# A two-layer decoder trunk on one core: v held in TensorE and the turned probabilities moved, so that y and its gates come out turned

## The chip, the cores and the metric

The kernel runs on one core of one Trainium2 chip. Its time is device microseconds of that core: 276.67 us, the median of three runs (276.58 to 276.71). Times below are read from one profiled execution of it.

## What is computed

One sequence of 256 positions with 1024 channels passes through two layers, with an RMS norm before each and after the last. All numbers are float32.

```python
def even_layer(hn, w_in, w_out, ln_g, ln_b, w_s, b_s):
    z = hn @ w_in
    u, v, g_a, q, k, vv, g_b = jnp.split(z, cuts, axis=-1)
    y_a = chunked_gmlp(u, v, ln_g, ln_b, w_s, b_s) * jax.nn.silu(g_a)
    y_b = moba_attention(q.reshape(hs), k.reshape(hs), vv.reshape(hs)).reshape(Bn, S, B_WIDTH)
    return jnp.concatenate([y_a, y_b * jax.nn.silu(g_b)], axis=-1) @ w_out

def odd_layer(hn, w_in, w_out):
    q, k, v, g = jnp.split(hn @ w_in, [C_WIDTH, 2 * C_WIDTH, 3 * C_WIDTH], axis=-1)
    y = dilated_mixture(q.reshape(hs), k.reshape(hs), v.reshape(hs)).reshape(Bn, S, C_WIDTH)
    return (y * jax.nn.silu(g)) @ w_out
```

With 256 positions the attention of the even layer (8 heads of 64 channels) is plain causal attention, and that of the odd layer (16 heads) is causal attention with a weight of 1, 2, 3 or 0 for each distance, which is a mask added to the scores.

## The kernel before

**Products.** Each of the four weight matrices is loaded in halves (512 rows by 512 columns, 1 MB) into three slots of `w_raw`. A quarter (two chunks of 128 rows) is split in two parts: ScalarE (ACT) copies it to `w_hi` in a rounded type (step `round`, L602) and VectorE (DVE) subtracts to get `w_lo` (step `rest`, L740). Nine quarters fit. TensorE (PE) makes each product of three: high by high, low by high, high by low. An item is one quarter for one group of two PSUM banks, and it is issued in two steps ("product n.0" and "n.1"), one for each chunk. Groups of kind value, gate, gelu and residual hold weights still and positions on partitions come out: hnT is stationary and 512 weight columns move (L1000 to L1002, six matmuls a chunk). Queries and keys come out turned, channels on partitions: the weights are stationary and the 256 positions move (L959 to L963, twelve matmuls a chunk).

**Attention of a head n** passes through these steps, each of which stands in the list of every engine that has a part in it: `scores` (four matmuls into a bank; then DVE adds the mask, scales and takes the least, L873; then ACT takes the exponential and the sum `den`, L652), `transpose` (PE turns three 128x128 blocks of `probs`, L911; ACT copies them to `probsT`, L660), and for every two heads `values` (PE, L1042 to L1044: turned probabilities stationary, 64 columns of v moving, six matmuls; DVE takes the reciprocal of the sums, L880, and multiplies by it into y, L882). Two `probs` buffers and two `probsT` buffers are used in turn. After four pairs `gating` multiplies y by the gate, and `y_pair` turns y for the output product: four transposes by PE, then ACT makes `yT_hi` (L664) and DVE `yT_lo` (L890).

**Order.** Nothing is scheduled at run time. `steps()` writes one list; each engine runs its own parts of that list in order and waits on semaphores. In the list, `HEADS_AT` sets after which product steps the parts of a head stand, `EVEN_AT` and `ODD_AT` the rest, and `LAST_ROUND` and `LAGS` how early the rounds and rests may be. `evacuate g` stands behind the last product of group g; for queries and keys it is four casts by ACT (L614) and four subtractions by DVE (L786), for gates a tanh by ACT (L634) and a multiplication by DVE (L793), each twice. Groups 1 and 2 are keys and queries of the even layer, 4 its attention gate; 11 and 12, 13 and 14 are queries and keys of the odd layer, 15 and 16 its gates. Groups of the even layer have four items each from item 0 on, groups 11 to 16 four each from item 60 on. Heads 8 to 15 are worked on beside items 69 to 78, heads 16 to 23 beside items 77 to 86.

## Time and profile before

| | us |
|---|---|
| median of three runs | 276.67 |
| the profiled execution: time | 275.13 |
| the profiled execution: span of the trace | 273.3 |
| PE busy | 261.1 |
| DVE busy | 179.3 |
| ACT busy | 159.1 |
| PE idle while it waits for another engine | 5.6 |

The times of steps come from the trace, with 0 at the start of its span. A row of the timeline gives start and length; matmuls overlap in it (a 128x512 one is shown as 0.39 us and the next begins 0.23 us after it), so the time that PE spends is read from start to start. One fp32 matmul (not of the rounded type) is shown as two rows.

### The profile page before, as it was taken

Reading aid. Unit: us, or ns where it says so; the run is one execution under the profiler, and the core shown is the slowest. Engines: PE = TensorE matmul, PEld = TensorE weight load, DVE = VectorE, ACT = ScalarE, POOL = GpSimd, SP = SyncE. Lnnn points to the kernel's source line nnn. Section 1 sums busy time; section 2 is a strip of 40 time slices with the busy share of each in tenths; the row PEclk is TensorE's granted clock in tenths of the full one; section 3 lists DMA queues with packets and bytes.
Section 4 is the critical chain, followed back from the end, with each engine's and each line's share of the span. In section 5 each row is a group of like instructions: output and inputs, shape, how many; then the busy total and the mean of one; then the engine's idle time right before and its main releaser. Section 6 shows DMA issues by size and latency. Waiting matters only on the chain.

```text
span 273.3 us, 4264 instructions
## 1 busy us (share of the span) xinstructions
PE 261.1 (96%) x1598; PEld 231.8 (85%) x1598; DVE 179.3 (66%) x327; ACT 159.1 (58%) x301; POOL 24.2 (9%) x52
## 2 busy tenths in 40 slices
PE   7999999959999999999999999999999999999990
PEld 6789997848888888887888999999998888988880
DVE  2975998967694788557758709393945858532643
ACT  4875857787466453637366646658666675640132
POOL 3016310000100000001100000200003001000021
PEclk9999999997999999999999999999999999999997
DMA  7999739482248144444447950735143441100004
GB/s 234 396 393 372 258 115 352 156 299 61 101 134 284 45 153 156 153 153 156 156 153 248 342 179 21 287 111 199 29 163 118 153 157 31 49 0 0 2 1 153
DMA packets 22452, 44.59 MB, mean 163 GB/s; under 512 B 1056, under 2 KB 1312, under 8 KB 22432
## 3 DMA queue, kind: packets, MB, share of 16 engines
q1 hardware_dynamic: 21712, 43.00, 45.7%
q10 hardware_dynamic: 576, 0.79, 0.8%
q0 software_dynamic: 144, 0.52, 0.6%
q8 instruction: 13, 0.21, 0.3%
q14 instruction: 7, 0.06, 0.1%
HBM read 43.26 MB, written 1.05 MB: 162 GB/s over the span
## 4 chain that ended last, share of the span: by engine, by line
PE 69%; DVE 13%; DMA 8%; ACT 5%; issue 3%; ACTq 0%; POOLq 0%; POOL 0%; DVEq 0%
PE products L1000 14%; PE products L1002 14%; PE products L1001 14%; DVE w_lo L740 6%; DMA w_raw<-in_ab_w_in 6%; PE products L963 5%; PE products L961 5%; PE products L959 5%; PE turned L911 3%; DVE k_low L786 3%; DMA y<-in_x_turned 2%; PE attended L1043 2%; PE attended L1044 2%; PE attended L1042 2%; PE scores L1020 1%
## 5 line engine op out<-in xcount | busy, mean ns | idle before, releaser
L740 DVE TENSOR_TENSOR w_lo<-w_raw,w_hi 128x1024 fp32r<-128x1024 f32 x74 | 89.0, 1227 | 9.8 <-ACT w_hi L602 9.1
L602 ACT CAST w_hi<-w_raw 128x1024 fp32r<-128x1024 f32 x74 | 75.9, 1047 | 31.3 <-PE products L1002 15.1
L959 PE MATMUL products<-hnT_hi,w_hi 128*128 128x256 f32 x192 | 54.7, 285 | 0.0
L963 PE MATMUL products<-hnT_hi,w_lo 128*128 128x256 f32 x192 | 54.3, 283 | 0.0
L961 PE MATMUL products<-hnT_lo,w_hi 128*128 128x256 f32 x192 | 54.3, 283 | 0.0
L1000 PE MATMUL products<-w_hi,hnT_hi 128*128 128x512 f32 x128 | 51.9, 405 | 0.1
L1002 PE MATMUL products<-w_lo,hnT_hi 128*128 128x512 f32 x128 | 50.5, 394 | 0.0
L1001 PE MATMUL products<-w_hi,hnT_lo 128*128 128x512 f32 x128 | 50.5, 394 | 0.0
L959 PEld LDWEIGHTS products<-hnT_hi,w_hi 128*128 128x128 f32 x192 | 36.7, 191 | 0.5 <-DVE w_lo L740 0.5
L961 PEld LDWEIGHTS products<-hnT_lo,w_hi 128*128 128x128 f32 x192 | 36.8, 192 | 0.0
L963 PEld LDWEIGHTS products<-hnT_hi,w_lo 128*128 128x128 f32 x192 | 36.7, 191 | 0.0
L652 ACT ACTIVATE probs<-probs,least 128x128 f32<-128x128 f32 (+1 forms) x48 | 21.4, 447 | 22.6 <-DVE least L873 22.6
L1002 PEld LDWEIGHTS products<-w_lo,hnT_hi 128*128 128x128 f32 x128 | 24.3, 190 | 5.3
L1000 PEld LDWEIGHTS products<-w_hi,hnT_hi 128*128 128x128 f32 x128 | 24.5, 191 | 4.7 <-issue 0.5
L1001 PEld LDWEIGHTS products<-w_hi,hnT_lo 128*128 128x128 f32 x128 | 24.4, 191 | 4.1
L1000 PE MATMUL products<-w_hi,yT_hi 128*128 128x512 f32 x64 | 25.6, 400 | 0.0
L1002 PE MATMUL products<-w_lo,yT_hi 128*128 128x512 f32 x64 | 25.0, 391 | 0.0
L1001 PE MATMUL products<-w_hi,yT_lo 128*128 128x512 f32 x64 | 24.9, 390 | 0.0
L660 ACT COPY probsT<-turned 128x384 f32<-128x384 f32 x24 | 11.4, 475 | 6.9 <-PE turned L911 6.8
L1002 PEld LDWEIGHTS products<-w_lo,yT_hi 128*128 128x128 f32 x64 | 12.0, 188 | 2.6
L557 ACT ACTIVATE tanh<-h 128x512 f32<-128x512 f32 x8 | 5.1, 632 | 15.5 <-DVE h L898 15.4
L1001 PEld LDWEIGHTS products<-w_hi,yT_lo 128*128 128x128 f32 x64 | 12.1, 188 | 2.3
(144 smaller groups left out, 361.3 us busy)
## 6 DMA issues: line engine op xcount, KB each, us to landing
w_raw<-in_c_w_in SPq DMA_DIRECT2D x16, 1024.0 KB, 5.5
w_raw<-in_ab_w_in SPq DMA_DIRECT2D x12, 1024.0 KB, 5.7
w_raw<-in_ab_w_out SPq DMA_DIRECT2D x4, 1024.0 KB, 5.0
w_raw<-in_c_w_out SPq DMA_DIRECT2D x4, 1024.0 KB, 5.0
w_raw<-in_ab_w_in SPq DMA_DIRECT2D x4, 256.0 KB, 4.9
w_raw<-in_ab_w_in SPq DMA_DIRECT2D x2, 512.0 KB, 7.7
h<-in_x SPq DMA_DIRECT2D x2, 512.0 KB, 11.1
out<-hn SPq DMA_DIRECT2D x4, 256.0 KB, 2.2
```

The source lines that it names most:

```text
L602: nc.scalar.copy(w_hi[:, n % SPLIT_SLOTS, :, :], w_raw[:, half % RAW_SLOTS, part, :]).then_inc(hi_ready, 1)
L652: last = nc.scalar.activation(probs[:, n % 2, a:b], probs[:, n % 2, a:b], ACT.Exp, scale=-1.0, bias=least[:, n, t:t + 1], accum_out=den[:, ...
L660: nc.scalar.copy(probsT[:, n % 2, :], turn_bank[:, 0:3 * P]).then_inc(probsT_ready, 1)
L740: nc.vector.tensor_tensor(w_lo[:, n % SPLIT_SLOTS, :, :], w_raw[:, half % RAW_SLOTS, part, :], w_hi[:, n % SPLIT_SLOTS, :, :].bitcast(fp32 ...
L786: last = nc.vector.tensor_tensor(to, bank[rows, :].rearrange("p (a b) -> p a b", b=SEQ), high.bitcast(fp32), ALU.subtract)
L911: return nc.tensor.matmul(to, of, ident[:], is_transpose=True, start=True, stop=True)
L959: nc.tensor.matmul(to, wh, hi[:, chunk, :], start=begins and c % 2 == 0, stop=False, skip_group_check=True)
L961: nc.tensor.matmul(to, wh, lo[:, chunk, :], start=False, stop=False, skip_group_check=True)
L963: last = nc.tensor.matmul(to, wl, hi[:, chunk, :], start=False, stop=ends, skip_group_check=True)
L1000: nc.tensor.matmul(to[:], xh, w_hi[:, slot, half_item, :], start=begins, stop=False)
L1001: nc.tensor.matmul(to[:], xl, w_hi[:, slot, half_item, :], start=False, stop=False)
L1002: last = nc.tensor.matmul(to[:], xh, w_lo[:, slot, half_item, :], start=False, stop=ends)
```

## The change

The sum of a head is divided out of the probabilities before they are turned: a new step `divide` on DVE takes the reciprocal of the two sums and multiplies `probs` by them in place. `probs` gets a third buffer. `transpose` waits for `divide` and no longer for the exponential alone. In `values` v is stationary (64 columns) and the turned probabilities move (256 columns for the first 128 keys, 128 for the second); the two heads of a pair write to partitions 0 to 63 and 64 to 127 of one bank, that is, they stand in the two halves of the columns of the PE array. DVE copies the result. y is so already turned, and its gates are made turned too: groups 4, 15 and 16 use the form of queries and keys. For the even layer DVE then scales such a gate by the norm of each position first (two instructions of 512 columns more), because the position no longer lies on partitions. Of the eight `y_pair` steps only the two of the gMLP keep their transposes on PE. `ones` moves into v, and the tables that set the order are new.

```diff
-LAST_ROUND = {2: 6, 3: 7, 4: 9, 5: 9, 6: 9, 7: 9, 8: 11, 9: 13, 10: 14, 11: 15, 12: 15, 13: 17, 14: 19, 15: 20}
-LAGS = {4: 0, 5: 0, 6: 0, 7: 0, 8: 1, 9: 1, 10: 1, 11: 0, 12: 4, 13: 4, 14: 1, 15: 1}
+LAST_ROUND = {2: 6, 3: 7, 4: 9, 5: 9, 6: 9, 7: 9, 8: 11, 9: 13, 10: 14, 11: 15, 12: 15, 13: 17, 14: 18, 15: 19, 16: 20,
+              17: 21, 18: 22, 19: 23, 20: 25, 21: 26, 22: 28, 23: 30}
+LAGS = {4: 0, 5: 0, 6: 0, 7: 0, 8: 1, 9: 1, 10: 1, 11: 1, 12: 4, 13: 4, 14: 1, 15: 1}
 HEADS_AT = (
-    ((10, 14, 19, 23),
-     (7, 9, 10, 12, 14, 17, 19, 21),
+    ((11, 15, 19, 23),
+     (8, 9, 11, 13, 15, 17, 19, 22),
+     (7, 8, 10, 12, 14, 16, 18, 21),
      (3, 3, 6, 9, 10, 12, 13, 17)),
-    ((9, 13, 15, 20),
-     (5, 7, 9, 10, 13, 14, 15, 18),
+    ((10, 13, 17, 21),
+     (6, 8, 9, 11, 13, 15, 16, 18),
+     (5, 7, 8, 10, 12, 14, 15, 17),
      (3, 4, 6, 7, 10, 10, 13, 14)),
-    ((8, 11, 14, 21),
-     (4, 5, 8, 9, 11, 12, 14, 17),
-     (3, 3, 4, 4, 9, 9, 13, 14)),
+    ((9, 12, 15, 20),
+     (6, 7, 9, 10, 12, 13, 16, 18),
+     (5, 6, 8, 9, 11, 12, 15, 17),
+     (3, 3, 4, 6, 9, 9, 13, 14)),
 )
 EVEN_AT = (
     (8, ("gelu_inner", 3)), (9, ("gelu_outer", 3)), (10, ("layer_norm", 0)), (13, ("layer_norm", 1)),
...
-    whole("even_in", gb, "gate", 1)
+    whole("even_in", gb, "gate_turned", 1)
...
-        whole("odd_in", 3 * D + c * BLOCK, "gate", c)
+        whole("odd_in", 3 * D + c * BLOCK, "gate_turned", c)
...
-        for stage, places in zip(("values", "transpose", "scores"), HEADS_AT[heads_set]):
+        for stage, places in zip(("values", "transpose", "divide", "scores"), HEADS_AT[heads_set]):
...
+                else:
+                    out.append(("rest", rounded.pop(0)))
...
-        probs = sb("probs", [P, 2, 3 * P])
+        probs = sb("probs", [P, 3, 3 * P])
...
+        def turned_y(n):
+
+            if n < EVEN_HEADS // 2:
+                return y[:, n // 2, BLOCK + (n % 2) * SEQ:BLOCK + (n % 2 + 1) * SEQ]
+            chunk = n - EVEN_HEADS // 2
+            return y[:, chunk // 4, (chunk % 4) * SEQ:(chunk % 4 + 1) * SEQ]
...
-                        act.wait_ge(rstd_parts, 2)
...
+                        act.wait_ge(rstd_parts, 3)
...
-                            last = nc.scalar.mul(v[:, t, 0:BLOCK], bank[:], rstd[:, t:t + 1])
+                            last = nc.scalar.mul(v[:, t, 0:BLOCK], bank[:], half_rstd[:, t:t + 1])
...
+                    elif kind == "gate_turned":
+
+                        act.wait_ge(dve_emptied, dve_emptied_before(n))
+                        for i, bank in enumerate(pair(n)):
+                            if n < FIRST_ODD:
+                                act.wait_ge(gate_scaled, i + 1)
+                            nc.scalar.activation(tanh[:, i, :], gate[:, place, i, :] if n < FIRST_ODD else bank[:],
+                                                 ACT.Tanh, scale=0.5).then_inc(tanh_ready, 1)
...
+                    if n in GMLP_PAIRS:
+                        act.wait_ge(y_turned, n - 1)
+                        source = bank[:]
+                    else:
+                        act.wait_ge(gated, n // 2 + 1)
+                        source = turned_y_pair(n)
...
+                elif what == "evacuate" and GROUPS_OF_BANKS[n][0] == "gate_turned":
+
+                    place = GROUPS_OF_BANKS[n][1]
+                    if n < FIRST_ODD:
+                        dve.wait_ge(products_done, LAST_ITEM_OF_GROUP[n] + 1)
+                        for i, bank in enumerate(pair(n)):
+                            nc.vector.tensor_tensor(
+                                gate[:, place, i, :].rearrange("p (a b) -> p a b", b=SEQ),
+                                bank[:].rearrange("p (a b) -> p a b", b=SEQ),
+                                rstd_rows[:].unsqueeze(1).to_broadcast([P, 2, SEQ]), ALU.mult).then_inc(gate_scaled, 1)
+                        dve.wait_ge(gate_scaled, 2)
+                    for i, bank in enumerate(pair(n)):
+                        dve.wait_ge(tanh_ready, tanh_writes_before(n) + i + 1)
+                        last = nc.vector.scalar_tensor_tensor(
+                            out=gate[:, place, i, :], in0=tanh[:, i, :], scalar=1.0,
+                            in1=gate[:, place, i, :] if n < FIRST_ODD else bank[:], op0=ALU.add, op1=ALU.mult)
+                    last.then_inc(dve_emptied, 1)
...
+                            part = y[:, t, BLOCK:D] if n == 0 else y[:, c, t * BLOCK:(t + 1) * BLOCK]
+                            last = nc.vector.tensor_tensor(part, part, gate[:, c, t, :], ALU.mult)
...
-                    if n >= 2:
-                        dve.wait_ge(probs_turned, n - 1)
+                    if n >= 3:
+                        dve.wait_ge(probs_turned, n - 2)
...
+                elif what == "divide":
+                    dve.wait_ge(probs_ready, n + 1)
+                    chain(nc.vector.reciprocal(den[:, n, :], den[:, n, :]), inverted, n + 1)
+                    for t, (a, b) in enumerate(((0, P), (P, 3 * P))):
+                        last = nc.vector.tensor_scalar(probs[:, n % 3, a:b], probs[:, n % 3, a:b], den[:, n, t:t + 1],
+                                                       None, ALU.mult)
+                    last.then_inc(probs_scaled, 1)
...
-                    chain(nc.vector.reciprocal(rden[:, pair_of, :], den[:, pair_of, :]), inverted, n + 1)
-                    column = value_column(2 * n) + (BLOCK if n < EVEN_HEADS // 2 else 0)
-                    nc.vector.tensor_tensor(
-                        y[:, :, column:column + 2 * HEAD].rearrange("p t (a d) -> p a t d", a=2),
-                        value_bank[:, 0:4 * HEAD].rearrange("p (a t d) -> p a t d", a=2, t=TILES),
-                        rden[:, pair_of, :].unsqueeze(3).to_broadcast([P, 2, TILES, HEAD]),
-                        ALU.mult).then_inc(attended, 1)
...
-                    if kind in ("query", "key"):
+                    if kind in ("query", "key", "gate_turned"):
...
-                    pe.wait_ge(probs_ready, n + 1)
+                    pe.wait_ge(probs_scaled, n + 1)
...
-                    for a in range(2):
-                        column = value_column(2 * n + a)
-                        pT = probsT[:, a, :]
-                        v0, v1 = v[:, 0, column:column + HEAD], v[:, 1, column:column + HEAD]
-                        first, second = (value_bank[:, (2 * a + t) * HEAD:(2 * a + t + 1) * HEAD] for t in range(2))
-                        nc.tensor.matmul(first, pT[:, 0:P], v0, start=True, stop=True)
-                        nc.tensor.matmul(second, pT[:, P:2 * P], v0, start=True, stop=False)
-                        last = nc.tensor.matmul(second, pT[:, 2 * P:3 * P], v1, start=False, stop=True)
+                    for tile, queries, of in ((0, slice(0, SEQ), slice(0, SEQ)), (1, slice(P, SEQ), slice(SEQ, 3 * P))):
+                        for a in range(2):
+                            column = value_column(2 * n + a)
+                            last = nc.tensor.matmul(value_bank[rows_of(a), queries], v[:, tile, column:column + HEAD],
+                                                    probsT[:, a, of], start=tile == 0, stop=tile == 1,
...
-                elif what == "y_pair":
+                elif what == "y_pair" and n in GMLP_PAIRS:
                     chunk, bank = y_place(n)
-                    pe.wait_ge(gated, n // 2 + 1)
-                    same_bank = [i for i in range(n) if y_place(i)[1] is bank]
-                    if same_bank:
```

What this makes of the order is shown at three places. In the odd layer group 13, the second half of the queries, ends with product 71.1. On DVE before, from the evacuation of that group on (`q_own<-products`), followed by a w_lo and by the reciprocal and product of heads 8 and 9:

```order
L786 TENSOR_TENSOR q_own<-products,q_own 64x2x256 x4
L740 TENSOR_TENSOR w_lo<-w_raw,w_hi 128x1024
L880 RECIPROCAL rden<-den 128x4
L882 TENSOR_TENSOR y<-attended,rden 128x2x2x64
L740 TENSOR_TENSOR w_lo<-w_raw,w_hi 128x1024
```

And on DVE now, where the first three-row piece after w_lo is the division of head 10, the copy of y is that of heads 8 and 9, and the second piece is head 11:

```order
L818 TENSOR_TENSOR q_own<-products,q_own 64x2x256 x4
L772 TENSOR_TENSOR w_lo<-w_raw,w_hi 128x1024
L922 RECIPROCAL den<-den 128x2
L924 TENSOR_SCALAR probs<-probs,den 128x128
L924 TENSOR_SCALAR probs<-probs,den 128x256
L772 TENSOR_TENSOR w_lo<-w_raw,w_hi 128x1024
L929 COPY y<-attended 128x256
```

The division of head 10 now stands behind the evacuation and a w_lo on DVE. On PE, beside it, the turn of head 10 stands one product step behind the end of group 13 (of the twelve matmuls of product 72.0 the last three are shown, then the turn of head 10 and the first of product 72.1; "..." stands for the others of it), and heads 8 and 9's values follow:

```order
L1003 MATMUL products<-hnT_hi,w_hi 128x256
L1005 MATMUL products<-hnT_lo,w_hi 128x256
L1007 MATMUL products<-hnT_hi,w_lo 128x256
L955 MATMUL turned<-ident,probs 128x128 x3
L1003 MATMUL products<-hnT_hi,w_hi 128x256
...
L1084 MATMUL attended<-probsT,v 64x256 x2
L1084 MATMUL attended<-probsT,v 64x128 x2
```

So the turn of head 10 comes before the values of heads 8 and 9, where before it came behind them. In the even layer, group 4 (the gate) ends with product 19.1. On DVE before, from the copy of y of a pair over the gate to the next mask:

```order
L880 RECIPROCAL rden<-den 128x4
L882 TENSOR_TENSOR y<-attended,rden 128x2x2x64
L793 SCALAR_TENSOR_TENSOR gate<-tanh,products 128x512 x2
L740 TENSOR_TENSOR w_lo<-w_raw,w_hi 128x1024
L873 ISA probs,least<-scores,mask_even 128x128
```

And on DVE now, where the division at the end is that of head 5, whose turn stands on PE behind product 20.0:

```order
L929 COPY y<-attended 128x256
L827 TENSOR_TENSOR gate<-products,rstd_rows 128x512 x2
L834 SCALAR_TENSOR_TENSOR gate<-tanh,gate 128x512 x2
L772 TENSOR_TENSOR w_lo<-w_raw,w_hi 128x1024 x2
L922 RECIPROCAL den<-den 128x2
L924 TENSOR_SCALAR probs<-probs,den 128x128
L924 TENSOR_SCALAR probs<-probs,den 128x256
```

Between the end of group 4 and that turn, DVE has gained the scaling of the gate, a w_lo and the division. In the even layer ACT's list has changed ahead of `gelu_inner` of group 3: before, nine rounds (16 to 24) stood between the evacuation of group 2 and it, now five (16 to 20).

## Rows read from the trace of the kernel before

**Rows 1.** The page: busy time of PE and DVE, then PE's granted clock.
```profile
PE 261.1 (96%) x1598; PEld 231.8 (85%) x1598; DVE 179.3 (66%) x327; ACT 159.1 (58%) x301; POOL 24.2 (9%) x52
...
PEclk9999999997999999999999999999999999999997
```
**Rows 2.** Who waited for whom on PE: total, times, longest.
```profile
PE attended L1042 <- ACT probsT L660: 2.9, 1, 2.9
...
PE scores L1019 <- DVE yT_hi L786: 0.6, 1, 0.6
```
**Rows 3.** The chain that ended last, 48 to 62 us: start, length, what.
```profile
52.63 5.39 DMA w_raw<-in_ab_w_in
...
58.99 1.26 ACT y L641 x2
```
**Rows 4.** Timeline of PE at 70 us (start, length): scores, products, values, a head's turn.
```profile
69.38 0.22 PE L1019 MATMUL scores<-yT_lo,yT_hi 128*128 128x128 f32 x1
...
69.83 0.40 PE L1000 MATMUL products<-w_hi,hnT_hi 128*128 128x512 f32 x1
...
71.21 0.33 PE L1042 MATMUL attended<-v,probsT 128*128 128x64 f32 x2
...
72.49 0.50 PE L911 MATMUL turned<-ident,probs 128*128 128x128 f32 x3
```
**Rows 5.** Timeline of PE at 17 us: twelve matmuls of a turned group apart.
```profile
17.81 0.28 PE L959 MATMUL products<-hnT_hi,w_hi 128*128 128x256 f32 x1
...
19.25 0.28 PE L959 MATMUL products<-hnT_hi,w_hi 128*128 128x256 f32 x1
```
**Rows 6.** Chain: four transposes of one y_pair, then gMLP's fp32 matmuls (two rows each).
```profile
233.44 0.44 PE attended L911 x4
...
83.69 0.89 PE scores L1052 x8
```
**Rows 7.** Windows 61 to 70 us (busy PE, PEld, DVE, ACT, POOL, PEclk) and a product there.
```profile
61.00:70.00 9.00, 9.00 (x48) 7.87 (x48) 6.42 (x18) 5.82 (x14) 1.25 (x2) 0.81 0.41 143
...
63.27 0.63 PE L1000 MATMUL products<-w_hi,hnT_hi 128*128 128x512 f32 x1
```
**Rows 8.** DVE groups by line and shape: count, busy us, mean ns, idle before.
```profile
L880 DVE RECIPROCAL rden<-den 128x4 f32<-128x4 f32 x12 | 2.1, 175 | 14.3 <-PE attended L1044 14.3
...
L696 DVE TENSOR_SCALAR gate<-gate 128x256 f32<-128x256 f32 x1 | 0.3, 293 | 0.0
```
**Rows 9.** Timeline of DVE: gelu_inner, a mask, then a layer norm up to 69.83.
```profile
59.71 1.28 DVE L802 SCALAR_TENSOR_TENSOR y<-y,products 128x512 f32<-128x512 f32 x2 [1.36 <-ACT y L641]
...
66.11 0.28 DVE L873 CUSTOM_DVE_ANT_0 probs<-scores,mask_even 128x128 f32<-128x128 f32 x1
...
66.66 0.69 DVE L819 BATCH_NORM_STATS2 moments<-hn 128x6 f32<-128x512 f32 x1
...
69.83 1.22 DVE L740 TENSOR_TENSOR w_lo<-w_raw,w_hi 128x1024 fp32r<-128x1024 f32 x1
```
**Rows 10.** Timelines of ACT and DVE at 76 us: the evacuation of the even gate.
```profile
76.01 1.26 ACT L634 ACTIVATE tanh<-products,half_rstd 128x512 f32<-128x512 f32 x2
...
78.27 1.27 DVE L793 SCALAR_TENSOR_TENSOR gate<-tanh,products 128x512 f32<-128x512 f32 x2
```
**Rows 11.** Timelines of PE, ACT and DVE at 188 us, the end of group 13.
```profile
188.51 0.28 PE L959 MATMUL products<-hnT_hi,w_hi 128*128 128x256 f32 x1
...
188.85 2.35 ACT L614 CAST q_own<-products 64x512 fp32r<-64x512 f32 x4
...
190.04 2.81 DVE L786 TENSOR_TENSOR q_own<-products,q_own 64x512 fp32r<-64x512 f32 x4 [2.12 <-ACT q_own L614]
192.88 1.23 DVE L740 TENSOR_TENSOR w_lo<-w_raw,w_hi 128x1024 fp32r<-128x1024 f32 x1
```
**Rows 12.** Timelines of PE and DVE at 207 us, the end of group 14.
```profile
207.36 0.40 PE L1000 MATMUL products<-w_hi,hnT_hi 128*128 128x512 f32 x1
...
208.87 2.81 DVE L786 TENSOR_TENSOR k_low<-products,k_own 64x512 fp32r<-64x512 f32 x4 [2.43 <-ACT k_own L614]
```

More of the change, by code:

```diff
@@ L135 @@
 LAST_ITEM_OF_QUARTER = {2 * item[1] + item[2]: n for n, item in enumerate(ITEMS)}
+GMLP_PAIRS = (2, 3)
 VALUE_KINDS = ("value", "value_tile")
 SPLIT_KINDS = ("query", "key")
+TANH_KINDS = ("gate", "gate_turned", "gelu")
 def steps():
@@ L263, in build @@
         rstd_rows = sb("rstd_rows", [P, SEQ])
-        ones = sb("ones", [P, P])
         hnT_hi = sb("hnT_hi", [P, CHUNKS, SEQ], fp32r)
@@ L295, in build @@
         meanvar = sb("meanvar", [P, TILES, nc.vector.BN_AGGR_DIM])
+        ones = v[:, 0, 0:P]
         gain = gate[:, 0, :, :].rearrange("p a b -> p (a b)")
@@ L374, in wait_emptied @@
             else:
-                engine.wait_ge(dve_emptied, count_of_kind(("gate", "gelu"), group))
+                engine.wait_ge(dve_emptied, count_of_kind(TANH_KINDS, group))
         def dve_emptied_before(group):
-            return count_of_kind(("gate", "gelu"), group - 1)
+            return count_of_kind(TANH_KINDS, group - 1)
         def tanh_writes_before(group):
@@ L452, in _ @@
         def _(pool):
-            nc.gpsimd.memset(ones[:], 1.0).then_inc(ones_ready, 1)
+            nc.gpsimd.memset(ones, 1.0).then_inc(ones_ready, 1)
             nc.gpsimd.memset(power[:], -0.5)
@@ L626, in _ @@
                     elif kind == "gate":
-                        if dve_emptied_before(n):
-                            act.wait_ge(dve_emptied, dve_emptied_before(n))
+                        act.wait_ge(dve_emptied, dve_emptied_before(n))
+                        act.wait_ge(rstd_parts, 4)
                         for t, bank in enumerate(pair(n)):
-                            half = half_rstd[:, t:t + 1] if n < FIRST_ODD else 0.5
-                            if t == 0 and n < FIRST_ODD:
-                                act.wait_ge(rstd_parts, 4)
-                            nc.scalar.activation(tanh[:, t, :], bank[:], ACT.Tanh, scale=half).then_inc(tanh_ready, 1)
+                            nc.scalar.activation(tanh[:, t, :], bank[:], ACT.Tanh,
+                                                 scale=half_rstd[:, t:t + 1]).then_inc(tanh_ready, 1)
+                    elif kind == "gate_turned":
+                        act.wait_ge(dve_emptied, dve_emptied_before(n))
+                        for i, bank in enumerate(pair(n)):
[3 more added lines that the diff above has]
+                                                 ACT.Tanh, scale=0.5).then_inc(tanh_ready, 1)
                 elif what == "gelu_inner":
@@ L921, in _ @@
             for _ in range(WARM):
-                nc.tensor.matmul(value_bank[:, 0:P], ones[:], ones[:], start=True, stop=True)
+                nc.tensor.matmul(value_bank[:, 0:P], ones, ones, start=True, stop=True)
             started = set()
```

36 lines of the change are left out of this document (17 added, 19 removed).

## The prediction

> **What bounds the kernel now.** The page first: PE is busy for 261.1 of 273.3 us, DVE for 179.3, and PE's granted clock is at its upper level (2.4 GHz) but for two slices [rows 1]. Next, who waited for whom: PE waited once for 2.9 us, for the turned probabilities of head 1, and once for 0.6 us; the rest of the waiting of the table ahead is at the start [rows 2]. So PE's own work sets the time, and another engine matters only where PE comes to wait for it. The chain at the one long wait shows why it is there: w_raw is loaded until 58.0, ACT's round of it stands ahead of gelu_inner, gelu_inner ahead of the copy of head 1's turn [rows 3].
>
> **The sum** is made against the profiled execution (span 273.3, time 275.13); the median of the runs is 276.67, 1.5 above it, and I add the difference to the median.
>
> **Gates made turned.** Twelve matmuls of a turned group take 19.25 - 17.81 = 1.44 us [rows 5], six of the other form 71.21 - 69.83 = 1.38 [rows 4]. Three groups of eight chunks: 24 x 0.06 = **+1.5**.
>
> **Transposes of y gone.** Six y_pairs of four transposes, 0.44 each [rows 6]: **-2.6**. What stays of them, ACT's cast and DVE's subtraction, is the same work from another source.
>
> **Values.** A pair takes 72.49 - 71.21 = 1.28 now, six fp32 matmuls of 64 columns, 0.213 each [rows 4]. The new four have 256, 256, 128 and 128 columns. The nearest row has fp32 matmuls of 128 columns: four in 0.89, 0.22 each, no more than those of 64 [rows 6]. So one end is four matmuls at 0.213, each two side by side in the halves of the array: 0.43. The other is that time goes with columns at the rate of that row: 768/128 x 0.22 = 1.33. The trace has nothing in half an array. I take 0.9, near the middle: -0.38 a pair, twelve pairs, **-4.6** (ends -10.2 and +0.6).
> The Trainium skill ("TensorEngine Tiling (Array Packing)", Key Properties) says that different tiles can load and multiply in parallel, and that a change of the tiling mode drains the engine. By the first the pair would come near the lower end; the second would add a drain on both sides of each pair. No run here shows either.
>
> **Waits of before that go.** ACT has five rounds ahead of gelu_inner where it had nine, so that copy no longer stands behind that load: -2.9. One w_lo moves behind the scaling of the queries, a w_lo is 1.2 us [rows 11], more than the 0.6 that the scores waited: -0.6. Together **-3.5**. Behind the long wait the clock was granted at 0.81 in the mean over 61 to 70 us, and a product that is otherwise shown as 0.40 took 0.63 [rows 7]: 9 x 0.19 = 1.7 us lost, as 3.4 us at the lower level (1.2 GHz): **-1.7**.
>
> So far -10.9. Against it stand the **new waits of PE**. A division needs DVE: a reciprocal 0.2, and two multiplications, of which 256 columns take 0.29 [rows 8]. Successive DVE instructions overlap by some 0.07, so I take 0.2 + 0.15 + 0.22 = 0.57 (at most 0.8). The 24 divisions add 13.7 us to DVE, the scaling of the even gate 1.3; DVE has the room in sum (179 of 273), but not at every place, since each engine keeps its order. Before, a head's turn needed nothing of DVE once it was masked. Now its division can stand behind long pieces:
>
> (a) *Even layer, end of the gate* (group 4). Behind the end of product 19.1 DVE scales the gate (two of 512 columns, 1.27 as the like pair [rows 10]), waits 0.2 for tanh, makes the gate (1.27), two w_lo (2.35) and the division of head 5 (0.57): 5.7 us. PE has one product of 1.38 until it needs that head. Wait **4.3**.
> (b) *Odd layer, end of the queries* (group 13), at 188.51. DVE is done with the evacuation at 192.85 because it follows ACT's casts, with w_lo at 194.0 [rows 11], with head 10 at 194.6. PE has a turn (0.33) and a product (1.44) and is there at 190.3. Wait **4.3**. Values of the pair before, which stood in between and hid ACT's share, now come behind.
> (c) *End of the keys* (group 14), at 207.36. DVE is done with the evacuation at 211.7 [rows 12], w_lo 212.9, a copy of y 0.35, head 15 at 213.8. PE has a turn, two products and a pair of values, 4.1 us. Wait **2.3**.
> (d) *End of gate 15*: evacuation 0.6 + 1.3 + 0.2 by the durations of [rows 10], w_lo 1.2, head 18 0.57: 3.9. PE: a product and a pair, 2.3. Wait **1.5**.
> (e) *Even layer from the mask of head 0 to the division of head 4.* DVE: seven masks at 0.55, six w_lo at 1.2, five divisions, gelu 4 x 0.63, two layer norms at 3.17, a copy [rows 9]: 23.0 us, and it waits for ACT's square as before (1.36 [rows 9]), for tanh alike. PE: products 6.9 + 10.1, six scores of 0.45 [rows 4], four turns, two pairs: 22.8. DVE starts 0.5 behind. The difference is 2.1 to 3.5; I take **3.5**, since a wait is not given back when DVE is later free.
>
> Together 15.9. The clock: PE had 2.9 us without work before its one fall inside the kernel. (a) and (b) are longer, so I charge two falls of 1.7: **+3.4**. The others may add up to two more.
>
> **Sum:** +1.5 - 2.6 - 4.6 - 3.5 - 1.7 + 15.9 + 3.4 = +8.4. The span would be 281.7, the median 285.1 us.
>
> **Rivals.**
> *The halves of the array don't overlap.* Values stay at 1.33, and each switch may cost: +5.2 against the forecast, less 1 that is then hidden ahead of (e): 289 to 291. For it: nothing in the trace ran so. Against: nothing either.
> *The halves overlap in full* (the rule of the skill's tiling page, named above): 0.43 a pair, -5.6 against the forecast, of which the pairs ahead of DVE-bound waits give back 1 to 2: 281. The sign stays.
> *DVE has more slack than I read.* (e) is made of many small pieces; if it falls away, and the clock falls but once, -5.2: 280.
> *Faster than before*, by one mechanism: the divisions are reached in time, so that PE doesn't wait at (a) and (b). This needs DVE to be through with evacuation, w_lo and division within the 1.4 and 1.8 us that PE has. It decides at 10.9: if new waits and the clock's falls stay below that, the kernel is faster. With (a), (b) and their falls gone the sum is -3.6, 273 us. Against it: DVE's rows at 190 to 194 are of the kernel as it is, with the same evacuation, and the order puts the division behind. For it: an overlap in full would leave only 5 us to be won back.
> *The change doesn't do what it says*: if the second half took no tile of its own, its matmuls would still write to partitions 64 to 127, at the first rival's price.
>
> **How the numbers follow.** Forecast with its bounds (waits 13 to 19, values 0.7 to 1.1): 281 to 289, chance 0.53. Full overlap or less waiting, 277 to 281: 0.16. No overlap, 289 to 292: 0.13. Within 0.2% of before (what a measurement of this kernel can tell from no change): 0.04. Faster: 0.14. The predicted time is that of the forecast, 285.1. The range of 8 in 10 leaves out the faster case and the far end of the slowest: 277 to 291.
>
> **What would show it.** PE's waits: rows of `turned` for DVE's new multiplication, of about 4 us at the ends of groups 4 and 13 and 2 at that of 14, and no row for head 1's turn of 2.9. Clock: a fall behind each of the long ones. Timeline: values 0.9 a pair; the second half beginning before the first ends shows the overlap. PE's list shorter by six groups of four transposes. The prediction is wrong if DVE's division rows at 194 come before the w_lo, or if PE's total of waits is under 9 us.

## The result and the profile after

The changed kernel takes 291.67 us (median of 4 runs, 290.88 to 292.41), the kernel before 276.69 (276.58 to 277.02): a ratio of 1.054, 95% interval 1.050 to 1.058. The forecast was 285.1 with 277 to 291 as its range. The sign is right, the size is not: 15.0 us came where 8.4 were expected, and the time lies above the range.

The profiled execution took 290.88 us, its span 288.8. From its page, the busy times and then PE's granted clock, as in [rows 1]:

```profile
PE 262.2 (91%) x1670; PEld 232.8 (81%) x1670; DVE 193.2 (67%) x389; ACT 159.6 (55%) x301; POOL 24.2 (8%) x52
...
PEclk9999999997979999999999999997799799999998
```

PE is busy for as long as before (262.2 against 261.1 us) in a span that is 15.5 us longer, DVE is busy 13.9 us longer, and the clock falls at four places inside the kernel instead of one. Who waited for whom on PE (total, times, longest), the counterpart of [rows 2]:

```profile
PE turned L955 <- DVE probs L924: 17.5, 8, 4.5
PE attended L966 <- POOL v L474: 1.0, 1, 1.0
PE attended L1084 <- ACT probsT L687: 0.9, 1, 0.9
PE products L1025 <- DVE hnT_lo L782: 0.5, 1, 0.5
```

The wait of 2.9 us of before is gone. In its place the turns wait eight times, 17.5 us in all, for L924, the multiplication of the new division. The even layer's heads lie at 50 to 95 us and the odd layer's at 182 to 245. The windows (length, PE busy, PEclk, DMA share, GB/s) show that the loss is there, first before, then after:

```profile
50.00:95.00 45.00, 42.08 (x233) 0.96 0.48 164
182.00:245.00 63.00, 62.59 (x439) 1.00 0.33 109
```
```profile
50.00:95.00 45.00, 36.84 (x232) 0.92 0.37 124
95.00:182.00 87.00, 85.95 (x497) 1.00 0.56 189
182.00:245.00 63.00, 54.57 (x425) 0.92 0.30 103
```

The two longest waits in the timelines (start, length; in brackets the idle time before and its releaser). Place (a), the end of the even gate, on DVE and then on PE:

```profile
75.93 1.29 DVE L827 TENSOR_TENSOR gate<-products,rstd_rows 128x512 f32<-128x512 f32 x2 [1.73 <-PE products L1007]
77.47 1.29 DVE L834 SCALAR_TENSOR_TENSOR gate<-tanh,gate 128x512 f32<-128x512 f32 x2 [0.26 <-ACT tanh L660]
78.69 2.35 DVE L772 TENSOR_TENSOR w_lo<-w_raw,w_hi 128x1024 fp32r<-128x1024 f32 x2
80.95 0.16 DVE L922 RECIPROCAL den<-den 128x2 f32<-128x2 f32 x1
81.15 0.55 DVE L924 TENSOR_SCALAR probs<-probs,den 128x128 f32<-128x128 f32 x2
```
```profile
76.89 0.39 PE L1046 MATMUL products<-w_lo,hnT_hi 128*128 128x512 f32 x1
81.75 0.44 PE L955 MATMUL turned<-ident,probs 128*128 128x128 f32 x2 [4.48 <-DVE probs L924]
```

Place (b), the end of the odd queries:

```profile
195.40 2.81 DVE L818 TENSOR_TENSOR q_own<-products,q_own 64x512 fp32r<-64x512 f32 x4 [2.12 <-ACT q_own L635]
198.24 1.23 DVE L772 TENSOR_TENSOR w_lo<-w_raw,w_hi 128x1024 fp32r<-128x1024 f32 x1
199.38 0.15 DVE L922 RECIPROCAL den<-den 128x2 f32<-128x2 f32 x1
199.57 0.55 DVE L924 TENSOR_SCALAR probs<-probs,den 128x128 f32<-128x128 f32 x2
```
```profile
200.18 0.90 PE L955 MATMUL turned<-ident,probs 128*128 128x128 f32 x3 [4.39 <-DVE probs L924]
200.73 0.56 PE L1003 MATMUL products<-hnT_hi,w_hi 128*128 128x256 f32 x1
```

The division is short, 0.75 us with its reciprocal. It is late because of what stands ahead of it on DVE: the evacuation and one or two w_lo. A product shown as 0.28 us in [rows 5] is shown as 0.56 here, the products behind that one as 0.41, and they begin 0.21 us apart and not 0.12. At each of its four longest waits (4.48, 4.39, 2.40 and 1.98 us) PE's clock falls to its lower level (1.2 GHz) for 3.4 us, at (b) for 6.8 us, of which 1.8 lie in the wait itself and 5.0 behind it. In windows of the changed kernel, (a)'s stretch, (b)'s, and the one behind it:

```profile
82.30:85.70 3.40, 3.40 (x11) 0.50 0.79 303
...
200.20:205.20 5.00, 5.00 (x24) 0.50 0.55 172
205.30:207.00 1.70, 1.70 (x16) 1.00 0.22 84
```

To see where the 15.5 us of span came from I split PE's time from each instruction's start to the next one's, by kind, took the idle time between PE's first and last instruction apart, and counted half of the time worked at the lower level as lost to the clock:

| us | forecast | measured |
|---|---|---|
| PE without work | -3.5 + 15.9 = +12.4 | 4.7 to 19.1: +14.4 |
| lost to the clock | -1.7 + 3.4 = +1.7 | 1.7 to 7.6: +5.9 |
| products (gates turned) | +1.5 | +2.7 |
| values | -4.6 | 15.6 to 9.8: -5.8 |
| turns of y | -2.6 | 2.9 to 0.7: -2.2 |
| the rest | 0 | +0.5 |
| sum | +8.4 | +15.5 |

The groups of the gates held hnT still and moved 512 weight columns before (the words "hold weights still" in the text on the kernel before are wrong there); now the weights are held and 256 positions move.

So my theory for the experiments: the places of the divisions on DVE make the waits, each long wait costs a fall of the clock on top, and the turned form itself gains. The rivals: DVE has too much work wherever the divisions stand; or the turned form (its gates, its halves) slows PE.

### The profile page after: what moved, and what is told of

The parts are those of the page before. It is cut to its first block, busy times and chain, and to the rows that moved or that the text cites. A ratio compares the mean times of both kernels' runs of the same rounds, so it can differ in the third digit from the quotient of the medians.

```text
span 288.8 us, 4464 instructions
## 1 busy us (share of the span) xinstructions
PE 262.2 (91%) x1670; PEld 232.8 (81%) x1670; DVE 193.2 (67%) x389; ACT 159.6 (55%) x301; POOL 24.2 (8%) x52
## 4 chain that ended last, share of the span: by engine, by line
PE 74%; DVE 15%; ACT 3%; DMA 3%; issue 2%; POOL 1%; POOLq 0%; DVEq 0%; ACTq 0%
PE products L1044 11%; PE products L1045 11%; PE products L1046 11%; PE products L1003 9%; PE products L1007 9%; PE products L1005 9%; DVE w_lo L772 5%; PE turned L955 3%; PE products L1025 3%; PE attended L1084 2%; PE scores L1063 2%; DVE k_low L818 2%; DMA w_raw<-in_ab_w_out 2%; PE scores L1064 2%; DVE probs L924 1%
## 5 line engine op out<-in xcount | busy, mean ns | idle before, releaser
L1003 PE MATMUL products<-hnT_hi,w_hi 128*128 128x256 f32 x288 | 84.5, 293 | 0.0
L1007 PE MATMUL products<-hnT_hi,w_lo 128*128 128x256 f32 x288 | 83.0, 288 | 0.0
L1005 PE MATMUL products<-hnT_lo,w_hi 128*128 128x256 f32 x288 | 82.9, 288 | 0.0
L1003 PEld LDWEIGHTS products<-hnT_hi,w_hi 128*128 128x128 f32 x288 | 56.7, 197 | 0.6 <-issue 0.5
L1005 PEld LDWEIGHTS products<-hnT_lo,w_hi 128*128 128x128 f32 x288 | 56.8, 197 | 0.1
L1007 PEld LDWEIGHTS products<-hnT_hi,w_lo 128*128 128x128 f32 x288 | 56.6, 197 | 0.0
L1044 PE MATMUL products<-w_hi,hnT_hi 128*128 128x512 f32 x80 | 32.5, 406 | 0.1
L1045 PE MATMUL products<-w_hi,hnT_lo 128*128 128x512 f32 x80 | 31.7, 396 | 0.0
L1046 PE MATMUL products<-w_lo,hnT_hi 128*128 128x512 f32 x80 | 31.7, 396 | 0.0
L955 PE MATMUL turned<-ident,probs 128*128 128x128 f32 x72 | 12.8, 288 | 17.5 <-DVE probs L924 17.5
L1044 PEld LDWEIGHTS products<-w_hi,hnT_hi 128*128 128x128 f32 x80 | 15.5, 193 | 3.5 <-issue 0.7
L1045 PEld LDWEIGHTS products<-w_hi,hnT_lo 128*128 128x128 f32 x80 | 15.5, 194 | 2.8
```

Of the source, the lines that this page charges most:

```text
L955: return nc.tensor.matmul(to, of, ident[:], is_transpose=True, start=True, stop=True)
L1003: nc.tensor.matmul(to, wh, hi[:, chunk, :], start=begins and c % 2 == 0, stop=False, skip_group_check=True)
L1005: nc.tensor.matmul(to, wh, lo[:, chunk, :], start=False, stop=False, skip_group_check=True)
L1007: last = nc.tensor.matmul(to, wl, hi[:, chunk, :], start=False, stop=ends, skip_group_check=True)
L1044: nc.tensor.matmul(to[:], xh, w_hi[:, slot, half_item, :], start=begins, stop=False)
L1045: nc.tensor.matmul(to[:], xl, w_hi[:, slot, half_item, :], start=False, stop=False)
```

## Experiments

Each ratio is taken against the kernel before on the same chip, where that took 275.0 to 276.2 us; the changed kernel's own ratio is 1.054. Not all kernels ran on the same chip, so differences between two of them are best read from their ratios.

**Four divisions earlier.**

```diff
-     (7, 8, 10, 12, 14, 16, 18, 21),
+     (7, 8, 10, 12, 14, 15, 18, 21),
...
-     (5, 7, 8, 10, 12, 14, 15, 17),
+     (5, 7, 7, 10, 12, 14, 15, 15),
...
-     (5, 6, 8, 9, 11, 12, 15, 17),
+     (5, 6, 7, 9, 11, 12, 15, 17),
```

> The changed kernel with four of its 24 divisions placed earlier among VectorE's steps, and nothing else: head 5's ahead of the evacuation of the even gates (place 16 to 15), head 10's ahead of that of the odd queries (8 to 7), head 15's ahead of that of the odd keys (17 to 15), head 18's ahead of that of gate group 15 (8 to 7). Theory (the waits come from where these divisions stand): TensorE's waits of 4.48, 4.39, 2.40 and 1.57 us are gone, and with the first three the lower clock level behind them (3.4, 6.8 and 3.4 us at half speed, so 1.7, 3.4 and 1.7 us of loss): 291.7 - 12.8 - 6.8 = 272 us, up to 276 if something else is late next; the fall behind the wait of 1.98 us at 65.5 us stays. Rival (VectorE simply has too much work, so that a wait removed here comes back at the next turn): 285 to 291 us. Rival (the turned form itself is slow on TensorE): 285 us or more with the waits gone.

Measured: 278.36 us, 1.007 of before (1.0035 to 1.0105). Four numbers in a table give back 13 of the 15 us. The four waits are gone, DVE's busy time is what it was (192.7 us), so the amount of work is not the cause. But 272 was not reached:

```profile
PE turned L955 <- DVE probs L924: 6.5, 5, 2.0
PE turned L955 <- ACT probsT L687: 3.0, 1, 3.0
PE attended L966 <- POOL v L474: 1.0, 1, 1.0
PE attended L1084 <- ACT probsT L687: 0.8, 1, 0.8
```

Place (b) has a second queue behind it. ACT's timeline there, then PE's:

```profile
190.03 2.35 ACT L635 CAST q_own<-products 64x512 fp32r<-64x512 f32 x4
192.41 1.04 ACT L623 CAST w_hi<-w_raw 128x1024 fp32r<-128x1024 f32 x1
193.48 0.48 ACT L687 COPY probsT<-turned 128x384 f32<-128x384 f32 x1
```
```profile
190.82 0.28 PE L1007 MATMUL products<-hnT_hi,w_lo 128*128 128x256 f32 x1
194.10 0.74 PE L955 MATMUL turned<-ident,probs 128*128 128x128 f32 x3 [3.01 <-ACT probsT L687]
```

ACT's copy of turn 9 stands behind its casts of the queries and a rounding, and turn 10 needs it. The division had only been later still. A fall of the clock at 194.3 followed, one at 68.0 behind turn 3 stayed, and turn 6 now waited 1.85 us, since its division stands behind the evacuation of the gates, three w_lo and a mask.

**No division.** The waiting and the three instructions of the division on DVE go, and the turn waits for the exponential.

```diff
-                    pe.wait_ge(probs_scaled, n + 1)
+                    pe.wait_ge(probs_ready, n + 1)
```

> The changed kernel with the division left out (the values are not divided by the sum); the turn waits for ScalarE's exponential alone. Theory (division behind other work): all of the 17.5 us that the turns waited for VectorE is gone, and all falls of the clock but the one at the end: 291.7 - 17.5 - about 7.5 = 265 to 268 us. Rival (something else than the division makes PE late, for instance the 256-column products or the values in two halves of the columns): 275 us or more, with waits of TensorE for other things in the place of these.

Measured: 271.72 us, 0.982 of before (0.977 to 0.988). PE no longer waits for DVE at the turns. The 265 to 268 are missed for the reason just seen:

```profile
PE attended L1079 <- ACT probsT L687: 3.4, 2, 3.0
PE turned L950 <- ACT probsT L687: 2.5, 1, 2.5
```

Two waits for ACT's copies, of 2.96 and 2.48 us, come up from under the divisions, each with a fall of the clock (at 87.9 and 190.3 us). With a short third they are 5.9 us of waiting, and the falls cost 3.4 more: together more than the miss.

**Division in its place, but short.**

```diff
-                    chain(nc.vector.reciprocal(den[:, n, :], den[:, n, :]), inverted, n + 1)
-                    for t, (a, b) in enumerate(((0, P), (P, 3 * P))):
-                        last = nc.vector.tensor_scalar(probs[:, n % 3, a:b], probs[:, n % 3, a:b], den[:, n, t:t + 1],
-                                                       None, ALU.mult)
-                    last.then_inc(probs_scaled, 1)
+                    nc.vector.reciprocal(den[:, n, :], den[:, n, :]).then_inc(probs_scaled, 1)
```

> The changed kernel with the two multiplications of each division left out (the values are not divided), the reciprocal and its place kept, and the turn waiting for it. It takes 0.62 us (0.55 and what lies between) from each of 24 divisions, 15 us of VectorE's work, and leaves every place as it is. Theory (the place is what costs): the waits of turns 5, 10, 15 and 18 shrink by 0.6 us each only, to 3.9, 3.8, 1.8 and 1.0, those of turns 2, 3 and 23 by as much; at least the falls behind the first two stay: 284 to 288 us. Rival (the amount of VectorE's work is what costs): the waits go nearly as without the division, 266 to 273 us.

Measured: 284.48 us, 1.030 of before (1.024 to 1.036), as the theory of the place had it.

```profile
PE turned L951 <- DVE den L922: 14.3, 8, 3.9
```

The four waits are 3.89, 3.80, 1.81 and 0.98 us, where 3.9, 3.8, 1.8 and 1.0 were expected. Taking 13 us of work from DVE shortens each of the four by 0.6; moving four steps takes them away. That tells place from amount.

**Work for PE in the waits.**

```diff
+                    if n in (5, 10, 15):
+                        bank = turn_bank if n == 15 else value_bank
+                        if n == 15:
+                            pe.wait_ge(probsT_ready, n)
+                        else:
+                            pe.wait_ge(attended, pairs_valued)
+                        for _ in range({5: 38, 10: 38, 15: 18}[n]):
+                            turn(bank[:, 3 * P:4 * P], ident[:])
                     pe.wait_ge(probs_scaled, n + 1)
```

> The changed kernel with turns of the identity that nothing reads added on TensorE ahead of its waits at turns 5 and 10 (38 each, about 3.3 us of a wait of 4.4) and at turn 15 (18, about 1.5 us of 2.4), so that TensorE works through most of the wait. VectorE's part is untouched, so the turns start when they did. Theory (each long idle stretch costs a fall of the clock on top of itself, 1.7 us for each 3.4 us at half speed, and 3.4 us behind turn 10): 291.7 - 6.8 = 284 to 286 us, and the granted clock doesn't fall at 82, 198 and 226 us; behind turn 3 (1.98 us at 65.5), where no turns are added, it still falls. Rival (the falls come from something other than idle time, or cost little since VectorE catches up in them): 290 to 292 us.

Measured: 286.15 us, 1.034 of before (1.029 to 1.039), just above the 284 to 286 expected and 5.5 us under the changed kernel, though it does 94 useless turns more and its divisions come no earlier. Windows over (a), the stretch behind it, (b), the stretch behind it, and the untouched wait of turn 3:

```profile
78.00:82.00 4.00, 3.86 (x36) 1.00 0.04 13
82.20:85.60 3.40, 3.40 (x19) 1.00 0.86 274
194.00:199.00 5.00, 4.76 (x44) 1.00 0.03 9
199.50:206.00 6.50, 6.50 (x57) 1.00 0.44 161
67.10:70.50 3.40, 3.35 (x16) 0.50 0.00 0
```

The clock stays up behind (a) and (b), where PE had worked through the wait, and falls behind turn 3, where it had not. In 3.40 us behind (a) PE now issues 19 instructions where the changed kernel had 11. The accounting says the same: 1.7 us lost to the clock against 7.6. So it is the idle time that brings the falls. All four of the changed kernel, that behind turn 3 included, cost 5.9 of the 15.5 us.

**Both heads in the same half of the columns.**

```diff
-                            last = nc.tensor.matmul(value_bank[rows_of(a), queries], v[:, tile, column:column + HEAD],
+                            cols = slice(a * SEQ + queries.start, a * SEQ + queries.stop)
+                            last = nc.tensor.matmul(value_bank[rows_of(0), cols], v[:, tile, column:column + HEAD],
```

Besides these lines, the matmuls that PE makes ahead of everything else (its first 18) write to two places in turn; they take as long as before (4.2 us).

> The changed kernel with the values of both heads of a pair written to the same 64 partitions (the second head to columns 256 to 511 of the bank), so that both use the same half of TensorE's columns; half of y is therefore not what it should be. Theory (the 0.80 us of a pair, against 1.30 before, come from the two halves working side by side, since the records of the two heads begin 0.01 us apart): the four matmuls of a pair run one after the other, 1.3 to 1.6 us a pair, 12 x 0.5 to 0.8 = 6 to 10 us more busy time, the waits as they are: 297 to 301 us. Rival (the pair is short because of moving 256 and 128 columns instead of six small matmuls, not because of the halves): 0.8 us a pair and 291 to 292 us.

Measured: 295.01 us, 1.070 of before (1.066 to 1.075); 3.3 more than the changed kernel by the medians, 4.6 by the ratios (5.4 by the spans, 294.2 and 288.8, of the slowest execution of the one and the fastest of the other) instead of 6 to 10, while the mechanism is as expected. One pair of values and what follows it, of the changed kernel and then of this one, both at the upper level:

```profile
210.85 0.87 PE L1084 MATMUL attended<-probsT,v 128*64 128x256 f32 x8
211.65 0.55 PE L955 MATMUL turned<-ident,probs 128*128 128x128 f32 x3
```
```profile
223.72 1.51 PE L1085 MATMUL attended<-probsT,v 128*64 128x256 f32 x8
225.17 0.39 PE L1003 MATMUL products<-hnT_hi,w_hi 128*128 128x256 f32 x1
```

211.65 - 210.85 = 0.80 against 225.17 - 223.72 = 1.45 a pair. All twelve take 17.5 us against 9.8: +7.8. What is given back: PE comes later to the divisions, so it waits for DVE 16.4 us and not 17.5 (0.5 less idle time in all), and the clock lost 4.3 us and not 7.6 in this execution, since the waits of 1.97 us at turn 3 and of 1.75 at turn 15 brought no fall. The products took 1.5 us more, for which I have no cause; with that the 5.4 us of span are accounted for within 0.1.

**The division without the turned form.** The kernel before with three buffers of probabilities, the divide step, and the changed kernel's table of places and of rounds; values, gates and y as before.

```diff
-                        ALU.mult).then_inc(attended, 1)
+                        value_bank[:, 0:4 * HEAD].rearrange("p (a t d) -> p a t d", a=2, t=TILES)).then_inc(attended, 1)
...
-                    pe.wait_ge(probs_ready, n + 1)
+                    pe.wait_ge(probs_scaled, n + 1)
```

> The kernel before with the other half of the change alone: the probabilities are divided ahead of the turn, at the changed kernel's places and with its three buffers of probabilities, its places of heads and its rounding table, while values, gates and y keep the form of before. Theory (the division's place makes the waits, and the turned form pays for itself): TensorE waits for VectorE about as long as in the changed kernel (17 to 19 us of idle time in all) with three to five lengths of the lower clock, and the values, the turns of y and the 512-column products are as before, so about 288.8 + 5.8 + 2.2 - 2.7 = 294 us of span, 293 to 297 us in time. Rival (the turned form, with its gates that VectorE scales on the way, makes the waits): 277 to 283 us.

Measured: 295.98 us, 1.076 of before (1.072 to 1.079), as expected.

```profile
PE turned L920 <- DVE probs L887: 16.9, 8, 4.4
```

Eight waits again, in a kernel that turns no gate and no value. So the division at these places, with the tables of places and rounds that came with it, costs about 20 us by itself, and the turned form gives some of them back: 4.3 us by the two times, 6.0 by the two ratios, 5.4 by the profiled spans (294.1 and 288.8).

**All waits placed earlier.**

```diff
-     (8, 9, 11, 13, 15, 17, 19, 22),
-     (7, 8, 10, 12, 14, 16, 18, 21),
+     (8, 9, 11, 13, 15, 17, 19, 21),
+     (7, 8, None, None, 12, 14, 15, 19),
...
-     (5, 7, 8, 10, 12, 14, 15, 17),
+     (5, 7, 7, 10, 12, 14, 15, 15),
...
-     (5, 6, 8, 9, 11, 12, 15, 17),
+     (5, 6, 7, 9, 11, 12, 15, 15),
...
-    (8, ("gelu_inner", 3)), (9, ("gelu_outer", 3)),
+    (8, ("gelu_inner", 3)), (9, ("divide", 2)), (9, ("divide", 3)), (9, ("gelu_outer", 3)),
```

> The changed kernel with every wait of 0.3 us or more among the heads given an earlier place: the four divisions of the first experiment (heads 5, 10, 15, 18), and besides those of heads 2 and 3 ahead of the outer gelu step of group 3, of 4, 6 and 7 by one or two places, of 23 ahead of gate group 16; turn 7 by one place, and ScalarE's copy of turn 9 ahead of its casts of the odd queries. In the first experiment the waits that were left sum to 10.4 us (1.44, 1.97, 0.34, 1.85, 0.83, 3.01, 0.95) with two falls of the clock of 1.7 us each behind those of 1.97 and 3.01. Theory: they go without another step becoming late, 276.4 - 10.4 - 3.4 = 262.6 us of span; with one or two new waits of 1 us, 263 to 268 us in time, 3 to 5% under the kernel before. Rival (VectorE has no slack left, work moved ahead makes masks, low parts of the weights or evacuations late): 272 to 278 us.

Measured: 268.92 us, 0.977 of before (0.974 to 0.980). That lies 0.9 us above the range given, 263 to 268, and below the rival's; no fall of the clock inside the kernel is left. ACT's copy of turn 9 is moved as well, as the next diff shows; the order of every other step is the changed kernel's. Waits that are left:

```profile
PE attended L1092 <- ACT probsT L695: 2.4, 2, 1.3
PE turned L963 <- DVE probs L932: 1.7, 1, 1.7
PE products L1033 <- DVE hnT_lo L790: 1.6, 1, 1.6
```

**ACT's copies too.** Four copies (that of turn 9 is in the experiment before already) ahead of what stood before them, for ACT alone, and one division for DVE alone.

```diff
+ACT_MOVES = ((("transpose", 9), ("evacuate", 13)), (("transpose", 2), ("scores", 4)), (("transpose", 3), ("scores", 5)),
+             (("transpose", 5), ("evacuate", 4)))
+DVE_MOVES = ((("divide", 11), ("evacuate", 13)),)
```

> The kernel of the experiment before with all waits placed earlier, and besides that ScalarE's copies of turns 2, 3 and 5 ahead of the exponentials of heads 4 and 5 and of the tanh of the even gates, and VectorE's division of head 11 ahead of the evacuation of the odd queries. TensorE's waits that were left there are 1.12 and 1.26 us (values 1 and 2, for ScalarE's copies) and 1.75 us (turn 11, for its division). Theory: 267.2 - 4.1 = 263.1 us of span, 264 to 266 us in time, no fall of the clock but the one at the end. Rival (what is moved delays the exponential, the tanh or the evacuation by as much): 268 to 271 us.

Measured: 267.13 us (267.04 to 267.27), 0.970 of before (0.966 to 0.975), span 265.2: between the two ranges, and only 1.8 us under the kernel with all waits placed earlier (1.9 by the ratios), where 4 were hoped for. The three waits named, 1.12, 1.26 and 1.75 us, are gone, but in their place stand 0.91 us at 72.4, 0.40 at 85.1 and 0.73 at 193.9: the next steps late.

**The kernel before, its own wait moved.**

```diff
+            act_order.remove(("transpose", 1))
+            act_order.insert(act_order.index(("round", 22)), ("transpose", 1))
```

> The kernel before, with one step of ScalarE moved: the copy of turn 1 ahead of its roundings 22 to 24, where before it stood behind them and behind the inner gelu step of group 3. Theory (every long wait of TensorE costs itself and a fall of the clock): the copy is done near 56.5 us instead of 60.6, the wait of 2.92 us for the first values is gone and with it the lower level at 62.4 to 65.8 us (1.7 us of loss): 273.3 - 2.9 - 1.7 = 268.7 us of span, 271 to 273 us in time. Rival (the roundings that it delays by 0.5 us each make the products wait, or the time is given back later): 275 to 278 us, the wait gone but others in its place.

Measured: 274.95 us, 0.998 of before (0.994 to 1.001): no difference. The wait moved, as the rival had it, in the form seen above:

```profile
PE turned L915 <- ACT probsT L664: 2.8, 1, 2.8
```

The copy of turn 1 is early, and then the copy of turn 2, behind the exponential, the tanh of 1.32 us and a rounding of 1.03, is late by as much; the fall of the clock comes behind that one (67.7 us instead of 62.4).

**Both copies moved, beside the turned form.**

```diff
+            act_order.remove(("transpose", 2))
+            act_order.insert(act_order.index(("scores", 3)), ("transpose", 2))
```

> The kernel before with two steps of ScalarE moved: the copy of turn 1 ahead of roundings 22 to 24, as in the experiment before, and the copy of turn 2 ahead of the exponential of head 3, so that it no longer stands behind that and the tanh of group 3 (there it ended at 66.5 us for a turn done at 60.6, and turn 3 waited 2.84 us for it). Theory: with both waits gone and no other, the 4.3 us idle falls to 1.5 and the fall of the clock goes: 274.4 - 2.8 - 1.7 = 269.9 us of span, 271 to 273 us in time; so the kernel before was itself held by one wait that moved rather than went. Rival (the wait moves on once more, to the exponential of head 3 or the gelu chain of group 3): 274 to 276 us.

> The fastest kernel so far (turned form, ten steps placed earlier) once more, beside the straight form with its own wait taken away, on the same chip. Theory: the turned form is worth values 15.6 - 9.6 and turns of y 2.9 - 0.7 less 2.7 of products, 5.5 us, when neither has a long wait: 267 us against 271 to 273. Rival (most of the gain over the kernel before was that kernel's own wait): the two within 1.5 us of each other.

Measured: the straight form 273.23 us, 0.993 of before (0.990 to 0.997), the turned form 267.05 (266.66 to 268.23), 0.970 (0.966 to 0.975). The straight form's wait moved once more, to 1.79 us for a mask at 66.7 us, again with a fall:

```profile
PE scores L1025 <- DVE least L879: 1.8, 1, 1.8
```

The sixteen steps placed otherwise (the "ten" of the text above is a miscount) leave 6.2 us between the two forms. Not all of that is the form's. The two profiled executions (spans 272.3 and 264.6) differ by 7.7 us, and split as above these are 0.8 of idle time (1.79 for the mask here, 0.90 and 0.72 left there), 1.7 of the clock, and the rest the work of PE: values 15.5 against 9.6, turns of y 2.9 against 0.7, products 2.9 the other way, 5.2 in sum. The execution that gives the straight form's median has a granted clock of 0.997, too high for a fall of 3.4 us; so, if the waits were those of the profiled ones, only the 0.8 of idle time is to be taken off the 6.2, which leaves 5.4. The form by itself is worth a little over 5 us here, as expected (5.5) and as the experiment on the division alone gave (5.4 by the spans).

## Why the prediction was off

The time came out above the range because the span's difference was 7.1 us larger than the sum: 4.2 from the clock, 2.0 from the waits, 1.2 from the products, 0.9 from smaller terms, less 1.2 from the values. The mechanism was right, and the term that failed by most is that of the clock.

- **What bounds the kernel, old waits gone.** Right: the wait of 2.9 us is gone, and so is that of 0.6.
- **New waits (a) to (d).** Right within 0.2 us each: 4.48 for 4.3, 4.39 for 4.3, 2.40 for 2.3, 1.57 for 1.5. The work was that of reading, in the order of steps, what stands ahead of the division on DVE and what PE has left. **(e)** came as turns 2, 3 and 4, 1.44 + 1.98 + 0.27 = 3.7 for 3.5. Its size is in part luck: it was worked out as one balance of DVE's work against PE's, and with all waits placed earlier the same work of DVE leaves none of the three waits, so it was the place here too.
- **Waits that I didn't list.** Turn 23 behind the evacuation of gate 16 (0.95) is the same pattern as (a) to (d) once more, and values 3 waited 0.94 for ACT's copy of turn 7, which stands behind a rounding that itself waited 2.88 us for its weights to be loaded. Together 1.9 us, the whole of what the waits' term lacked.
- **The clock: the term that was mis-sized.** The text charged "two falls of 1.7: +3.4", with "The others may add up to two more" left out of the sum. There were four inside the kernel, of 3.4, 3.4, 6.8 and 3.4 us in order of time: behind turn 3, (a), (b) and (c), that at (b) of double length. Part of the double one fell into the wait itself, so 7.6 us were lost and not 3.4: 4.2 of the 7.1 by which the span's difference was too small. Charging all four and none double would have given 288.5. The experiment with work for PE in three of the waits shows the price: with their falls gone, 1.7 us are lost and not 7.6.
- **Values.** Side by side, as hoped: the records of the two heads begin 0.01 us apart (59.32 and 59.33 for the first pair). A pair takes 0.80 us where 0.9 was taken: -5.8 for -4.6. That 0.9 was near is luck, since both of its ends were wrong in one of two things: the halves do overlap nearly in full (half of the 1.45 us in one half is 0.73), and the time does go with the columns (1.45 against the 1.33 worked out from them), so the 0.43 of the rival with full overlap was out of reach. The Trainium skill ("TensorEngine Tiling (Array Packing)", Key Properties) says that different tiles can work in parallel; 0.80 against 1.45 bears it out. A drain at each change of the mode, its other rule, can't be told apart in the 0.80.
- **Gates made turned.** The sums by kind give 1.50 us for twelve matmuls of the 24 turned chunks and 1.39 for the six of before, so 0.11 for each and not the 0.06 of one pair of rows: +2.7 for +1.5. The rows were rightly read: chunks that follow one another still take 1.44 us. But the gates' chunks stand among steps of attention, and behind such a step one takes some 1.52, in the kernel before too (1.52 at 183 us, 1.51 at 206): its first matmul, behind a turn, begins 0.20 ahead of the next and not 0.12. A mean over all of the kernel before (1.45 and 1.40) would have given only +1.2.
- **Turns of y.** -2.2 for -2.6: four turns issue in 0.37 us; the row's 0.44 has the last one's end in it.
- **The range.** 291.67 lies just above the price of the rival without overlap (289 to 291), and was reached by another mechanism. The unknown sizes of values went into the range, the falls "up to two more" hardly did, although the four that came cost 4.2 us more than was charged, against 3 us on either side for all the waits (13 to 19).

## What to carry to other kernels

When a step is added to an engine that has time to spare in sum, its price is set by what stands ahead of it in that engine's queue at the moment the critical engine needs it; here four table entries decided 13 us, and 13 us of work some 7. Each wait that is taken away uncovers the next queue that the same step hangs on (DVE's division, then ACT's copy), so all of them are to be read before one is moved. And a long idle stretch of PE is to be charged with its fall of the clock as a matter of course: it is the largest part, 4.2 of 7.1 us, of what this forecast lacked.

## What the runs showed of the chip

Over the profiled executions of all kernels here, 15 waits of PE between 2.1 and 4.5 us were each followed by the lower level, twelve times for 3.4 us and three times for 6.8; of ten between 1.75 and 2.1 us five were (1.98, 1.97, 1.81, 1.98 and 1.79, but not 1.97, 2.06, 1.85, 1.75 and 1.75); none under 1.7 us was. A wait near 2 us is thus worth itself or 1.7 us more, and which of the two isn't settled by its length alone: that of 1.97 us at turn 3 brought a fall in the kernel with four divisions earlier and none in that with both heads in one half. It differs between executions of one kernel too. Of the ten with four divisions earlier, eight had a mean granted clock of 0.981 to 0.986 and took 277.3 to 280.5 us, two had 0.993 and took 276.4 and 276.7. Of the kernel before on that chip, eleven of thirteen had 0.982 to 0.984 (275.8 to 278.0 us) and two 0.987 and 0.989 (275.3 and 275.0); the execution profiled here is of the second sort (0.989), so most of the others may hold one fall more, of which there is no trace. Useless turns of the identity kept the level up at all three places where they filled most of the wait. Two fp32 matmuls of 64 stationary columns in different halves of the columns ran side by side at little loss: 0.80 us a pair of heads against 1.45 in one half, half of which would be 0.73.
